# A two-block transformer kernel on one core: gate products of a gated head moved to its front, its state products regrouped, and residual additions done block by block

## What is computed

```python
def gla_log_gate(h, w1, w2, b):
    return jax.nn.log_sigmoid(((h @ w1) @ w2 + b).astype(jnp.float32)) / GLA_TAU
...
    def step(s, inp):
        qc, kc, vc, gc = inp
        G = jnp.cumsum(gc, axis=2)
        G_last = G[:, :, -1:, :]
        q_t = qc * jnp.exp(G)
        k_t = kc * jnp.exp(-G)
        a = jnp.where(mask, jnp.einsum('bhid,bhjd->bhij', q_t, k_t), 0.0)
        o = jnp.einsum('bhij,bhjv->bhiv', a, vc) + jnp.einsum('bhid,bhdv->bhiv', q_t, s)
        k_end = kc * jnp.exp(G_last - G)
        s_new = jnp.exp(G_last[:, :, 0, :])[..., None] * s + jnp.einsum('bhjd,bhjv->bhdv', k_end, vc)
...
        return (y * jax.nn.silu(h @ w_r)) @ w_o
...
        x_lat = x_lat + m_lat[:, 2] * rms_norm(y_lat, norm_g[i, 1])
        h = modulate(rms_norm(x_lat, norm_g[i, 2]), m_lat[:, 3], m_lat[:, 4])
        x_lat = x_lat + m_lat[:, 5] * rms_norm(sqrelu_mlp(h, mlp_w1[i], mlp_w2[i]), norm_g[i, 3])
```

## Time and profile before

| what | value |
|---|---|
| median of the runs (3) | 3810.27 us |
| lowest and highest | 3809.92 and 3813.37 us |
| the profiled execution's own time | 3819.68 us |
| its span | 3818.0 us |
| PE busy | 3542.8 us, 93% of the span |
| DVE busy | 1894.3 us, 50% |
| ACT busy | 1192.5 us, 31% |
| mean granted TensorE clock | 0.966 of 2.4 GHz |

### The profile page before, as it was taken

One profiled execution on the slowest core, in us unless ns is written; L12 is line 12 of the kernel. 1 busy time (PEld: TensorE's weight loads), 2 busy tenths in 40 slices (PEclk: granted clock), 3 DMA queues, 4 the chain that ended last, 5 costly groups with the idle time before them and its releaser, 6 DMA issues.

```text
span 3818.0 us, 45316 instructions
## 1 busy us (share of the span) xinstructions
PE 3542.8 (93%) x17054; PEld 2828.6 (74%) x17054; DVE 1894.3 (50%) x2705; ACT 1192.5 (31%) x1541; POOL 202.1 (5%) x372
## 2 busy tenths in 40 slices
PE   7999879999987998899989999799999999899998
PEld 3566679999985777677846656668876777678876
DVE  4555546345446445644435655566744343345433
ACT  3133434213224233433323333233323222333332
POOL 0110001001000000111100000011100000000000
PEclk9999989999998989999999999899999999999999
DMA  6211114333320111344421111035533222222222
GB/s 208 78 60 58 50 36 130 96 104 116 105 75 28 37 48 54 122 154 154 156 73 34 33 44 44 13 130 176 176 120 95 69 75 66 66 78 93 94 83 82
DMA packets 294716, 335.20 MB, mean 88 GB/s; under 512 B 16465, under 2 KB 264145, under 8 KB 294481
## 3 DMA queue, kind: packets, MB, share of 16 engines
q1 hardware_dynamic: 261552, 232.93, 19.1%
q0 software_dynamic: 29440, 96.49, 7.8%
q10 hardware_dynamic: 3617, 4.26, 0.3%
HBM read 331.55 MB, written 2.10 MB: 87 GB/s over the span
## 4 chain that ended last, share of the span: by engine, by line
PE 85%; DVE 6%; ACT 3%; DMA 3%; issue 2%; DVEq 0%; ACTq 0%; SPq 0%; POOLq 0%; POOL 0%
PE acc L724 62%; PE sc L724 6%; PE sc L1278 2%; DMA wring<-in_mlp_w 1%; PE sc L758 1%; PE acc L936 1%; PE sc L852 1%; PE acc L1278 1%; PE sc L916 1%; PE acc L1456 1%; PE sc L755 1%; PE sc L918 1%; DVE w_lo L2250 1%; DVE arena L2007 1%; PE acc L1156 1%
## 5 line engine op out<-in xcount | busy, mean ns | idle before, releaser
L724 PE MATMUL acc<-x_lo,w_hi 128*128 128x512 f32 (+1 forms) x2144 | 806.0, 376 | 31.3 <-DVE d_out_lo L2227 9.2
L2250 DVE TENSOR_TENSOR w_lo<-wring,w_hi 128x1024 fp32r<-128x1024 f32 (+2 forms) x400 | 441.8, 1146 | 584.2 <-ACT w_hi L1636 584.1
L1636 ACT ACTIVATE w_hi<-wring 128x1024 fp32r<-128x1024 f32 (+2 forms) x400 | 377.4, 991 | 1037.2 <-DMA wring<-in_mlp_w 480.8
L724 PEld LDWEIGHTS acc<-x_lo,w_hi 128*128 128x128 f32 x2144 | 406.4, 190 | 95.6 <-DVE w_lo L2250 25.9
L724 PE MATMUL acc<-hid_hi,w_hi 128*128 128x512 f32 (+1 forms) x1120 | 414.4, 370 | 28.2 <-DVE arena L2285 14.1
L724 PE MATMUL acc<-hid_hi,w_lo 128*128 128x512 f32 (+1 forms) x1120 | 411.4, 367 | 0.0
L724 PE MATMUL acc<-x_hi_holes,w_hi 128*128 128x512 f32 x704 | 278.6, 396 | 11.4 <-DVE x_lo L2256 9.0
L724 PE MATMUL acc<-x_hi_holes,w_lo 128*128 128x512 f32 x704 | 278.7, 396 | 0.0
L724 PE MATMUL acc<-hid_lo,w_hi 128*128 128x384 f32 (+1 forms) x768 | 272.8, 355 | 0.0
L724 PEld LDWEIGHTS acc<-hid_hi,w_hi 128*128 128x128 f32 x1120 | 213.0, 190 | 56.7 <-DVE arena L2285 17.0
L724 PE MATMUL acc<-x_hi_seq,w_hi 128*128 128x512 f32 x576 | 227.8, 395 | 11.5 <-DVE x_lo L2259 9.0
(11 more groups left out here) (400 smaller groups left out, 5928.3 us busy)
## 6 DMA issues: line engine op xcount, KB each, us to landing
wring<-in_mlp_w SPq DMA_DIRECT2D x64, 1024.0 KB, 5.4
rows_or_mod<-in_ada_w POOLq DMA_DIRECT2D x208, 256.0 KB, 3.2
wring<-in_ffn_up SPq DMA_DIRECT2D x44, 1024.0 KB, 5.0
wring<-in_ret_w_in SPq DMA_DIRECT2D x24, 1024.0 KB, 5.2
rstd<-in_ada_w POOLq DMA_DIRECT2D x88, 256.0 KB, 3.4
wring<-in_ffn_down SPq DMA_DIRECT2D x32, 704.0 KB, 4.5
wring<-in_gdn_w_in SPq DMA_DIRECT2D x16, 1024.0 KB, 5.7
tab<-in_ada_w POOLq DMA_DIRECT2D x40, 256.0 KB, 3.4
```

What stands on the lines that cost most here:

```text
L724: ins = pe.matmul(o, lhsT, rhs, start=start, stop=stop)
L1636: f(w_hi[s][:, c], wring[s][:, c], ACT.Copy).then_inc(w_high, 1)
L2250: tt(w_lo[s][:, c], wring[s][:, c], w_hi[s][:, c].bitcast(F32), SUB).then_inc(w_split, 1)
```

## The change

It has three parts. In a GLA head of the loop (heads 1 to 3) the two gate products come first, as units 0 and 1, then query (2) and key (3); ACT and DVE do their work in the order that fits. In all heads the state products are regrouped (units 10 and 11 hold four states of a direction each, unit 12 the fifth of both), the output is one unit (13, was 14 and 15) with all products of `g_AT` ahead of all products of the states, the mask of unit 9 (`copy_predicated`) is written ahead of the state recurrence, and `gate_columns(1)` stands behind the first eight state products in the loop and right behind `gate_columns(0)` in head 0. A product of unit 12 raises `w_used` in place of the next head's first query product. Last, `residual` goes block by block, and `add_square` no longer trails by one block.

```diff
-    ("gla_head", 4, 4, 16), ("gla_out", 1, 4, 8),
+    ("gla_head", 4, 4, 14), ("gla_out", 1, 4, 8),
...
-    def settle(self):
+    def settle(self, but=0):
...
+                        begun[0] = stage != "gla_out"
...
+                def gates(j):
+                    pe.wait_ge(gate2_in, it * 32 + 32)
+                    for d in range(2):
+                        claim(pe, S, it, j + d)
+                        rows = slice(d * GATE_AT, d * GATE_AT + GATE_RANK)
+                        for h in range(2):
+                            last = pe.matmul(unit(S, j + d)[:, h, 0:HALF], gate2[rows, :],
+                                             hgate[rows, h * HALF:(h + 1) * HALF], start=True, stop=True)
+                        last.then_inc(acc_ready, 1)
...
+                    pe.wait_ge(g1_moved, 1)
+                    gates(2)
                 else:
+                    gates(0)
                     for j in range(2):
                         w = split_group(S, it, j, DB, P)
-                        claim(pe, S, it, j)
+                        begun[0] = j == 1
+                        claim(pe, S, it, 2 + j)
...
                 gate_columns(0)
+                if first:
+                    gate_columns(1).then_inc(gr_ready, 1)
...
+                emptied(pe, S, it, 6)
                 for d in range(2):
                     emptied(pe, S, it, 7 + d)
...
+                    claim(pe, S, it, 10 + d)
+                    for i in range(4):
+                        last = states(d, i, unit(S, 10 + d)[:, i // 2, (i % 2) * 256:(i % 2) * 256 + 256])
                     last.then_inc(acc_ready, 1)
+                if not first:
+                    gate_columns(1).then_inc(gr_ready, 1)
+                claim(pe, S, it, 12)
+                states(0, 4, unit(S, 12)[:, 0, 0:256]).then_inc(w_used, 1)
+                states(1, 4, unit(S, 12)[:, 1, 0:256]).then_inc(acc_ready, 1)
+
+                claim(pe, S, it, 13)
+                toks = [(b, t, slice(t * P, (t + 1) * P), slice(b * P, (b + 1) * P)) for b in range(2) for t in range(LT)]
+                for b, t, tok, v in toks:
+                    o = unit(S, 13)[:, b, tok]
+                    pe.matmul(o, g_v[:, 2 + t, v], g_AT[:, 0, tok], start=t == 0, stop=False)
+                    pe.matmul(o, g_v[:, 2 + t, v], g_AT[:, 1, tok], start=False, stop=False)
+                emptied(pe, S, it, 12)
+                for b, t, tok, v in toks:
+                    o = unit(S, 13)[:, b, tok]
+                    pe.matmul(o, g_S[:, 0, 1 + t, v], g_qS[:, 0, tok], start=False, stop=False)
+                    last = pe.matmul(o, g_S[:, 1, 4 - t, v], g_qS[:, 1, tok], start=False, stop=t == LT - 1)
+                last.then_inc(acc_ready, 1)
...
                 deviation_of(name)
+                st.did(tt(y[:, 0], y[:, 0], rstd[:, 0:n], MUL))
                 for b in range(DB):
-                    st.did(tt(y[:, b], y[:, b], rstd[:, 0:n], MUL))
-                st.settle()
-                for b in range(DB):
+                    if b + 1 < DB:
+                        st.did(tt(y[:, b + 1], y[:, b + 1], rstd[:, 0:n], MUL))
+                    st.settle(int(b + 1 < DB))
...
-                    if j >= 2:
-                        add_square(name, j - 1, n)
+                    if 1 <= j < 7:
+                        add_square(name, j, n)
...
-                            if last and u >= 10:
-                                add_square(f"y{i}m", u - 9, n)
+                            for b in {13: (1, 2, 3, 4), 14: (5, 6)}.get(u, ()) if last else ():
+                                add_square(f"y{i}m", b, n)
...
+                else:
+                    gates()
+                    decays(0)
+                    decays(1)
+                    split_weights(S, it, 2)
+                    decayed(0)
+                    values(0)
+                    split_weights(S, it, 3)
+                    decayed(1)
+                    values(1)
+                    head_out(slice(2 * GLA_H - 4, 2 * GLA_H - 2) if final else bass.ds(it * 2 - 2, 2), it * 1)
+                    values(2)
+
+                finished(dve, S, it, 9)
+                dve.memset(g_mark, 0.0)
+                free(dve.copy_predicated(g_AT.rearrange("p d (t n) -> p d t n", n=P), tri,
+                                         unit(S, 9).rearrange("p d (t n) -> p d t n", n=P)), S, 9)
...
+                finished(dve, S, it, 13)
+                free(cp(g_o, unit(S, 13)), S, 13)
```

More of the change, by code:

```diff
@@ L133, in did @@
             self.local += 1
-    def settle(self):
-        v = self.n if self.it is None else self.it * self.per + (self.n + self.local)
+    def settle(self, but=0):
+        v = self.n - but if self.it is None else self.it * self.per + (self.n + self.local - but)
         self.eng.wait_ge(self.sem, v)
@@ L1093, in gla_head @@
                     head_sum(it * 1)
[L1095 to L1104, removed]
                 w = split_group(S, it, 2, DB, GLA_DV)
@@ L1146, in gla_head, with states @@
                 last.then_inc(acc_ready, 1)
+                def states(d, i, o):
+                    t = order[d][i]
+                    return pe.matmul(o, g_kEt[:, d, i * P:(i + 1) * P], g_v[:, t, :], start=True, stop=True)
+                emptied(pe, S, it, 6)
                 for d in range(2):
                     emptied(pe, S, it, 7 + d)
[L1150 to L1173, removed]
-                    last.then_inc(acc_ready, 1)
+                    claim(pe, S, it, 10 + d)
@@ L1726, in gla_head, with queries, keys, logs @@
             def gla_head(it, first, final):
[L1728 to L1738, removed]
-                    st.settle()
[L1740 to L1743, removed]
+                q, k, z = (0, 1, 2) if first else (2, 3, 0)
+                def queries():
+                    finished(act, S, it, q)
+                    free(f(g_q, unit(S, q)[:, 0, :], ACT.Copy, scale=P ** -0.5), S, q)
+                def keys():
+                    finished(act, S, it, k)
+                    free(f(halves(g_k), unit(S, k)[:, :, 0:HALF], ACT.Copy), S, k)
+                def logs():
+                    for d in range(2):
+                        l = g_ke[:, d, :]
+                        emptied(act, S, it, z + d)
+                        st.did(f(l, g_z[:, d, :], ACT.Abs))
+                        st.settle()
+                        st.did(f(l, l, ACT.Exp, scale=-1.0))
+                        st.settle()
+                        f(l, l, ACT.Ln, bias=1.0).then_inc(gl_ready, 1)
+                def decays(d):
                     act.wait_ge(gG_ready, it * 2 + d + 1)
@@ L1748, in gla_head @@
                     f(g_et[:, d, :], g_tot[:, d, :], ACT.Exp, scale=1 / 16).then_inc(gE_ready, 1)
-                    if d == 0:
-                        high_weights(S, it, 3)
+                if first:
+                    queries()
+                    high_weights(S, it, 2)
+                    keys()
+                    logs()
+                    decays(0)
+                    high_weights(S, it, 3)
+                    decays(1)
+                else:
+                    logs()
+                    queries()
+                    decays(0)
+                    high_weights(S, it, 2)
+                    keys()
+                    decays(1)
+                    head_deviation(it * 1)
+                    high_weights(S, it, 3)
                 for d in range(2):
@@ L2332, in gla_head, with gates @@
             def gla_head(it, first, final):
[L2334 to L2339, removed]
+                q, k, z = (0, 1, 2) if first else (2, 3, 0)
+                def gates():
+                    for d in range(2):
+                        finished(dve, S, it, z + d)
+                        free(ts(halves(g_z[:, d, :]), unit(S, z + d)[:, :, 0:HALF], dyncol("gla_b_gate", it * 1 + 4 * d), None, ADD), S, z + d)
                 def values(j):
@@ L2343, in values, with decays @@
                     free(cp(g_v[:, 2 * j:2 * j + 2, :], unit(S, 4 + j)[:, :, 0:GLA_DV]), S, 4 + j)
-                for d in range(2):
-                    emptied(dve, S, it, 2 + d)
+                def decays(d):
+                    emptied(dve, S, it, z + d)
                     dve.wait_ge(gl_ready, it * 2 + d + 1)
@@ L2410, in gla_head @@
                 dve.wait_ge(g_done, it * 1 + 1)
-                for b in range(2):
-                    finished(dve, S, it, 14 + b)
-                    free(cp(g_o[:, b, :], unit(S, 14 + b)[:, 0, :]), S, 14 + b)
+                finished(dve, S, it, 13)
+                free(cp(g_o, unit(S, 13)), S, 13)
                 if not final:
```

53 lines of the change are left out of this document (29 added, 24 removed).

## The result

The changed kernel takes 3770.21 us (median of 4 runs, 3768.72 to 3771.23), the kernel before beside it 3811.82 (4 runs, 3809.92 to 3818.16): ratio 0.9888 [0.9871, 0.9905], 41.6 us less. The forecast was 23.5 less, 3787, range 3776 to 3799. The sign was right; the gain is 1.8 times the sum, and outside the range.

What follows compares the result with a forecast made beforehand. PE was taken to bound the kernel (85% of the chain), so only its waits counted. Residual places 15.3 plus heads 8.2 gave 23.5 us off the 3810.3 median: 3786.8, forecast 3787, range 3776 to 3799.

Steps and rivals of the forecast that it cites:

- The added sum (all four places): Sum of squares after the last projection: earlier additions let its first half follow at once; 3.0, 1.9, 0.8, 0.8 us.
- Residual places: The four residuals with the sums ahead of them: earlier sums and first blocks save 15.3 us together.
- A: Residual ahead of the first MLP: 3.3 us sooner, limited by DVE's memset and split ahead of the norm.
- B: Residual between the first MLP and GLA head 0: 6.3 us sooner, 1.9 of it from the earlier sum.
- C: Residual between the output projection and the second MLP: 1.9 us sooner, limited by DVE's queue.
- D: Residual after the second MLP, with no memset: 3.8 us sooner (bounds 0 and 4.5).
- Heads: The four GLA heads: 15.6 us of PE waits removed, less 1.0, 5.8 and 0.6 of new costs, net 8.2.
- rival 2: Front of each looped head: the stall lets the clock fall, 3 us per head, 9 in all; 3796, chance 0.15.
- 3: GLA heads: DVE late with the values' split or scaled keys, so the heads give nothing; 3795, chance 0.08.
- 4: Residual sums: PE, paced by DVE, stays at 1.2 GHz; residuals −7, heads +8, no change; 3809, chance 0.07.
- 5: GLA heads: the stretch of small fp32 products falls to 1.2 GHz, costing up to 55 us; 3842, chance 0.04.
- 6: Whole kernel: fewer waits also spare clock falls that the timed runs had; 3776 to 3780, chance 0.06.

Runs made afterwards that it cites:

- the second profile: The kernel before, unchanged, run and profiled again: 3814.72 us, ratio 1.0003 [0.9991, 1.0014].

## Why the prediction was right or wrong

**The step that failed** is "The added sum (all four places)". It said that "the additions are done earlier (under units 13 and 14 of the MLP, or under the next projection unit), so the first half of the sum follows the projection at once", and costed only that end. It never asked what the first addition had waited for where it stood, nor what was queued behind it. Inside the MLPs the first addition in fact moved later, from unit 10 to 13, and that took waits of 18.7 and 10.5 us out of DVE's queue, and with them two stalls of PE, 16 us in all. With them the sum is 39.5, against 41.6 measured. That it comes so near is not proof of each term: the heads gave more than their 8.2, and the timed parts (16 for the heads, 17 to 23 for the additions in the MLPs, 3 to 6 for the loop) scatter by several us. I looked up PE's waits only at the places that I had already chosen; two rows of that list, 14.1 and 9.5, longer than any in the earlier trace rows, lay in stages where a moved line stood.

**Residual places, 15.3: right in sum, in part by luck.** A, from ten products before the end of the projection to 100 products into the MLP: 58.0 and 57.2 in the two profiles of before, 54.6 after, so 2.6 to 3.4 for 3.3. But 1.6 of that term is the eight records of 4.48, which take 2.85 in the second profile and in that of the kernel with only the new additions in the MLPs, so that fall of the clock was chance. Up to the MLP's first product A gives 3.4 against the first profile and only 1.4 against the second, whose MLP then starts more slowly. B, from the last projection product's end to the norm's first multiplication: 35.4 before, 29.5 after, 6.0 for 6.3. C: 1.9 to 2.6 for 1.9. D: from DVE's last instruction of the MLP's sum to the second unit's first product 27.55 before, 23.20 after, 4.35 for 3.8. The split was off: the block order gave 6 to 7 by stage for 9.5, and the rest must be the additions, 5.8 in the forecast. The 1.9 in B is shown by itself (41.4 for 43.4); in A, C and D no run has the additions alone.

**Heads, net 8.2: too small.** The removed 15.6 went, the late mask brought 7.2 of them back, the new stall came at the forecast place and size (2.0 a head for 1.9). At two fronts of three the clock fell as well (rival 2 in part, 1.6 in each of those two, not 3 in all three). Yet 10.9 is measured against the second profile of before (1.3 in head 0, 9.6 in heads 1 to 3), 18.1 against the first, and 16 timed. What the old profiles differ by goes with their time at the lower clock. The 2.7 above the forecast does not: the looped heads of the second one stood 6.8 us at the lower clock, as the new ones do. Where those 2.7 come from stays open. The Trainium skill, page "TensorE: Matmul & The Clock Gate", section "A second HAM failure mode: psum-queue depth-cycling", speaks of brief repeated idling that swings the clock; the windows agree (0.67 and 0.61 behind stalls of some 2 us), though one front in three stayed at 1.00.

**Rivals.** 3: no wait for the values' split. 4: PE was paced by DVE at full clock in B after the first blocks (its 2.56 is right as four records of 0.64; the six products in 3.0 beside it include two that only reach into the window). 5: the stretch of small products stayed at 1.00 in head 0. 6, spared clock falls, may be part of the heads' timed gain, which no run isolates. I discounted head 2's stretch at 0.50 as chance; it is not in the second profile of before, so that was right, but falls of some kind stood in each of the three.

## What to carry to other kernels

When a diff moves an instruction on a queue, price the move at both ends: what the instruction waited for where it stood, and what stood behind it there. An instruction that waits for a second engine inherits the first thing in that engine's queue, here a weight load. Then go through the list of waits of the bounding engine from the top and ask of each large row whether a moved line lies in its stage.

## What was new of the hardware

- Waits of PE cost more here than their length. A gap of 6 us in the first MLP cost about 8, since PE came back at a granted clock of 0.61; waits of 5.4 us in three heads cost 7.3, with 3.4 us more at the lower clock.
- The kernel before scatters more (medians 3812 to 3818, single runs 3806 to 3828) than the changed one (medians 3770 and 3771, single runs 3769 to 3775, but only eight of them). Three profiles with its heads show clock falls at different points of them; with the new heads, in eight profiles, they stand at two of the three fronts each time (heads 1 and 3 in seven of them, 2 and 3 in one). Whether that is the whole cause of the scatter stays open.
